# Four output projections with a norm in pieces: the norm of a token tile let out over the following items, and its residual fetched in eight slices

## What is computed

```python
for i in range(DEPTH):                                   # 4 layers
    shift, scale, gate = ada_modulation(c, w_ada[i], b_ada[i])
    h = rms_norm(x, g_norm[i]) * (1.0 + scale) + shift
    ...                                                  # input projection and mixer of layer i: y, z
    out = jnp.einsum('bse,ed->bsd', y * jax.nn.silu(z), w_out)
    x = x + gate * out
return rms_norm(x, g_final), ...
```

## Time and profile before

| | |
|---|---|
| runs, median (lowest to highest) | 2855.18 us (2853.37 to 3117.13) |
| profiled execution, time | 2853.27 us |
| its span, slowest core (core 2) | 2851.7 us (other cores from 2838.4) |
| PE busy | 2253.8 us, 79% |
| DVE busy | 1498.8 us, 53% |
| ACT busy | 778.4 us, 27% |
| mean granted PE clock, 8 cores | 0.913 to 0.920 |
| DMA, mean rate | 75 GB/s |
| chain that ended last, by engine | PE 58%, DVE 19%, ACT 10%, issue 6%, DMA 5% |

### The profile page before, as it was taken

One profiled execution on the slowest core, in us unless ns is written; L12 is line 12 of the kernel. 1 busy time (PEld: TensorE's weight loads), 2 busy tenths in 40 slices (PEclk: granted clock), 3 DMA queues, 4 the chain that ended last, 5 costly groups with the idle time before them and its releaser, 6 DMA issues.

```text
span 2851.7 us, 38831 instructions; the slowest of 8 cores (2838.4 to 2851.7 us)
## 1 busy us (share of the span) xinstructions
PE 2253.8 (79%) x12651; PEld 1200.2 (42%) x12651; DVE 1498.8 (53%) x2600; ACT 778.4 (27%) x1381; POOL 198.4 (7%) x373
## 2 busy tenths in 40 slices
PE   1396899977899999878688888867578687685976
PEld 0142555543455555443345454533243343341543
DVE  1466562233666666533566666567633444757343
ACT  2621233333311111132322222256522322121211
POOL 1001201100010101000000000000000100000000
PEclk9998899988999999988799998988788899897998
DMA  9300727534343433424543334234433421111132
GB/s 185 98 1 4 119 34 130 85 100 103 55 63 50 60 52 52 78 80 125 103 78 78 78 78 78 60 83 116 112 110 115 83 31 27 23 27 15 49 110 86
DMA packets 142851, 215.10 MB, mean 75 GB/s; under 512 B 14560, under 2 KB 83168, under 8 KB 141920
## 3 DMA queue, kind: packets, MB, share of 16 engines
q0 software_dynamic: 50544, 96.00, 22.8%
q1 hardware_dynamic: 92112, 116.63, 13.4%
HBM read 255.18 MB, written 53.40 MB: 108 GB/s over the span
## 4 chain that ended last, share of the span: by engine, by line
PE 58%; DVE 19%; ACT 10%; issue 6%; DMA 5%; POOL 1%; DVEq 1%; ACTq 0%; SPq 0%; POOLq 0%
PE ps L458 37%; PE ps L569 15%; DVE big L1027 4%; ACT big L526 3%; DVE big L516 2%; ACT big L953 2%; DVE big L681 2%; DVE big L1032 2%; ACT big L1012 2%; PE ps L508 2%; PE ps L879 1%; DVE big L915 1%; DMA big<-w_ada 1%; DVE big L524 1%; DMA big<-xbuf 1%
## 5 line engine op out<-in xcount | busy, mean ns | idle before, releaser
L458 PE MATMUL ps<-big 128*128 128x384 bf16 (+4 forms) x7360 | 1417.7, 352 | 206.7 <-ACT big L1012 104.4
L458 PEld LDWEIGHTS ps<-big 128*128 128x128 bf16 x7360 | 723.9, 100 | 841.0 <-issue 305.2
L569 PE MATMUL ps<-big 128*128 128x384 bf16 (+4 forms) x2560 | 522.7, 363 | 20.7 <-DVE big L966 20.7
L569 PEld LDWEIGHTS ps<-big 128*128 128x128 bf16 x2560 | 263.6, 103 | 255.8 <-issue 70.7
L577 DVE SCALAR_TENSOR_TENSOR big<-ps,big 128x384 f32<-128x384 f32 (+3 forms) x192 | 110.2, 582 | 406.6 <-PE ps L569 376.4
L507 ACT ACTIVATE big<-big 128x384 bf16<-128x384 f32 (+4 forms) x200 | 107.9, 554 | 510.1 <-DVE big L577 463.0
L508 PE MATMUL ps<-big 128*128 128x384 bf16 (+4 forms) x200 | 75.3, 397 | 211.3 <-ACT big L507 211.3
L915 DVE TENSOR_TENSOR big<-big,ps 128x384 bf16<-128x384 f32 (+1 forms) x96 | 160.1, 1668 | 106.0 <-ACT big L911 103.0
L526 ACT ACTIVATE big<-big 128x384 bf16<-128x384 f32 (+3 forms) x192 | 131.3, 684 | 94.8 <-DVE big L524 78.6
L1027 DVE TENSOR_TENSOR big<-big 128x398 f32<-128x398 f32 (+11 forms) x200 | 121.9, 610 | 57.6 <-ACT big L1012 42.4
L674 PE MATMUL ps<-big 128*128 128x512 bf16 (+1 forms) x576 | 129.2, 387 | 10.0 <-ACT big L677 5.4
(11 more groups left out here) (105 smaller groups left out, 1678.9 us busy)
## 6 DMA issues: line engine op xcount, KB each, us to landing
big<-w_ada POOLq DMA_DIRECT2D x96, 256.0 KB, 6.6
big<-w_in_b POOLq DMA_DIRECT2D x64, 256.0 KB, 6.6
big<-w_in_c POOLq DMA_DIRECT2D x48, 256.0 KB, 5.4
big<-xbuf SPq DMA_DIRECT2D x7, 1536.0 KB, 8.9
xbuf<-big SPq DMA_DIRECT2D x48, 192.0 KB, 2.0
gbuf<-big SPq DMA_DIRECT2D x16, 548.0 KB, 6.3
big<-gbuf SPq DMA_DIRECT2D x16, 548.0 KB, 4.9
ybuf<-big SPq DMA_DIRECT2D x16, 540.0 KB, 2.7
```

The lines of the kernel that those rows point to most:

```text
L458: ins = h.matmul(out, lhsT=lhs(k), rhs=rhs(k), start=(k == 0), stop=(k == n - 1))
L569: ins = h.matmul(bank(b)[:, 0:w], lhsT=w8[e // 8][:, e % 8, :], rhs=YS[:, e, x0:x0 + w], start=(e == 0), stop=(e == 15))
```

## The change

The L508 of every item now comes two items later. There are four `SQ` buffers, and one buffer `RB` for the reciprocal in place of two. The norm of a tile is a list of nine `chores`: Sqrt and reciprocal, then eight pieces, one a slice (`h_piece`, or `y_piece` in the last projection), each of which also issues the fetch of its slice for tile t + 2. `tick` takes up to three chores after every item, so a norm lasts over three items. The last tile's norm goes on in the first items of the next layer; `proj` empties the list before it reads the last tile. The first two tiles are fetched in eight slices each as well. In layer_c the load of the table `wtab` is deferred by nine items, not three.

```diff
-    RB = [Buf("rb%d" % i, NRM_o + i * 512, 512) for i in range(2)]
-    SQ = [Buf("sq%d" % i, NRM_o + 1024 + i * 256, 512, True) for i in range(2)]
+    RB = Buf("rb", NRM_o, 512)
+    SQ = [Buf("sq%d" % i, NRM_o + 512 + i * 256, 512, True) for i in range(4)]
...
-    def tick():
+    chores = []
+
+    def tick(k=3):
         for e in later:
             e[0] -= 1
         while later and later[0][0] <= 0:
             later.pop(0)[1]()
+        for _ in range(k):
+            if chores:
+                chores.pop(0)()
 
     def flush():
-        while later:
-            later.pop(0)[1]()
+        while later or chores:
+            if later:
+                later.pop(0)[1]()
+            else:
+                chores.pop(0)()
...
+    nsq = [0]
+
     def sumsq(t, d, w):
         q = t % 2
-        k = d % 2
+        S = SQ[nsq[0] % 4]
+        nsq[0] += 1
...
     def rstd(t, w):
+        b = 6 + t % 2
+        s.op("act", lambda h: h.activation(out=RB.v[:, 0:w], in_=bank(b)[:, 0:w], func=AF.Sqrt, bias=EPS, scale=1.0 / D), reads=[], writes=bk(b) + [RB.key])
+        s.op("dve", lambda h: h.reciprocal(out=RB.v[:, 0:w], in_=RB.v[:, 0:w]), reads=[RB.key], writes=[RB.key])
...
+    def h_piece(l, t, d, x0, w, sg):
+        X = XT[t % 2][d]
+        s.op("dve", lambda h: h.tensor_tensor(out=X.v[:, 0:w], in0=X.v[:, 0:w], in1=RB.v[:, 0:w], op=ALU.mult), reads=[RB.key, X.key], writes=[X.key])
+        for (a, b, sq) in sg:
+            s.op("act", lambda h, a=a, b=b, sq=sq: h.activation(
+                out=HT[:, d, 80 + a:80 + b], in_=X.v[:, a - x0:b - x0], func=AF.Identity, scale=gsv(l)[:, d, sq:sq + 1], bias=modv(l)[:, d, sq:sq + 1]),
+                reads=[X.key, "gs%d" % l, "mod%d" % l], writes=["hT.%d" % t])
...
+    def y_piece(t, d, x0, w):
         q = t % 2
-        b = 6 + q
-        R = RB[q]
-        s.op("act", lambda h: h.activation(out=R.v[:, 0:w], in_=bank(b)[:, 0:w], func=AF.Sqrt, bias=EPS, scale=1.0 / D), reads=[], writes=bk(b) + [R.key])
-        s.op("dve", lambda h: h.reciprocal(out=R.v[:, 0:w], in_=R.v[:, 0:w]), reads=[R.key], writes=[R.key])
-        return R
+        X = XT[q][d]
+        s.op("dve", lambda h: h.scalar_tensor_tensor(out=X.v[:, 0:w], in0=X.v[:, 0:w], scalar=gfin[:, d:d + 1], in1=RB.v[:, 0:w],
+                                                     op0=ALU.mult, op1=ALU.mult), reads=[RB.key, X.key, "par"], writes=[X.key])
+        s.dma("sp", "xo%d.%d" % (q, d), yt_d[d][:, x0 - HALO:x0 - HALO + w], X.v[:, 0:w], reads=[X.key], writes=["O.y.%d.%d" % (t, d)])
...
     def make_h(l, t, x0, w, sg):
-        q = t % 2
-        R = rstd(t, w)
+        rstd(t, w)
         for d in range(8):
...
-    def make_y(t, x0, w):
+            h_piece(l, t, d, x0, w, sg)
...
-        if l == 0:
-            src = xt_d[:, :, 80 + x0:80 + x0 + w]
-            rd = []
-        else:
-            src = xbuf[:, :, x0:x0 + w]
-            rd = ["XD.%d.%d" % (t, d) for d in range(8)]
-        s.dma("sp", "xl%d" % q, XTall[q][:, :, 0:w], src.rearrange("d p n -> p d n"), reads=rd, writes=XTK[q])
+        s.dma("sp", "xl%d" % q, XTall[q][:, :, 0:w], xt_d[:, :, 80 + x0:80 + x0 + w].rearrange("d p n -> p d n"), reads=[], writes=XTK[q])
...
+    def load_piece(t, d, x0, w):
+        q = t % 2
+        s.dma("sp", "xi%d.%d" % (q, d), XT[q][d].v[:, 0:w], xbuf[d][:, x0:x0 + w], reads=["XD.%d.%d" % (t, d)], writes=[XT[q][d].key])
+
+    def load_first(t, d, x0, w):
+        q = t % 2
+        s.dma("sp", "xi%d.%d" % (q, d), XT[q][d].v[:, 0:w], xt_d[d][:, 80 + x0:80 + x0 + w], reads=[], writes=[XT[q][d].key])
...
-        load_x(l, 0, *geo[0])
-        load_x(l, 1, *geo[1])
+        fetch = load_first if l == 0 else load_piece
+        for t in range(2):
+            for d in range(8):
+                fetch(t, d, *geo[t])
+
+        def norm(t):
+            x0, w = geo[t]
+            sg = segs(t, lo)
+            chores.append(lambda: rstd(t, w))
+            for d in range(8):
+                def piece(d=d):
+                    if l < 3:
+                        h_piece(l + 1, t, d, x0, w, sg)
+                    else:
+                        y_piece(t, d, x0, w)
+                    if t + 2 < NT:
+                        fetch(t + 2, d, *geo[t + 2])
+                chores.append(piece)
...
-                last = (d == 7)
-
-                def after(st=st, last=last, t=t, x0=x0, w=w, sg=sg):
+
+                def after(st=st, last=(d == 7), t=t):
                     st()
                     if last:
-                        if l < 3:
-                            make_h(l + 1, t, x0, w, sg)
-                        else:
-                            make_y(t, x0, w)
-                        if t + 2 < NT:
-                            load_x(l, t + 2, *geo[t + 2])
-                defer(1 if d < 7 else 2, after)
+                        norm(t)
+                defer(2, after)
...
     def proj(l, idx, t, lo=0):
         x0, x1 = max(TB[t], lo), TB[t + 1]
+        if t == NT - 1:
+            while chores:
+                chores.pop(0)()
...
-        defer(3, lambda: s.dma("pool", "wtab", wt_b.v, wtab_d, writes=["wtab"]))
+        defer(9, lambda: s.dma("pool", "wtab", wt_b.v, wtab_d, writes=["wtab"]))
```

More of the change, by code:

```diff
@@ L501, in segs @@
         return [(x0, SMP, 0), (SMP, x1, 1)]
+    nsq = [0]
     def sumsq(t, d, w):
         q = t % 2
-        k = d % 2
+        S = SQ[nsq[0] % 4]
+        nsq[0] += 1
         b = 6 + t % 2
-        s.op("act", lambda h: h.activation(out=SQ[k].v[:, 0:w], in_=XT[q][d].v[:, 0:w], func=AF.Square), reads=[XT[q][d].key], writes=[SQ[k].key])
-        return lambda: s.op("pe", lambda h: h.matmul(bank(b)[:, 0:w], lhsT=onesb, rhs=SQ[k].v[:, 0:w], start=(d == 0), stop=(d == 7)),
-                            reads=["onesb", SQ[k].key], writes=bk(b))
+        s.op("act", lambda h: h.activation(out=S.v[:, 0:w], in_=XT[q][d].v[:, 0:w], func=AF.Square), reads=[XT[q][d].key], writes=[S.key])
+        return lambda: s.op("pe", lambda h: h.matmul(bank(b)[:, 0:w], lhsT=onesb, rhs=S.v[:, 0:w], start=(d == 0), stop=(d == 7)),
+                            reads=["onesb", S.key], writes=bk(b))
@@ L530, in make_y @@
-    def make_y(t, x0, w):
-        q = t % 2
-        R = rstd(t, w)
-        for d in range(8):
-            X = XT[q][d]
-            s.op("dve", lambda h, X=X, d=d: h.scalar_tensor_tensor(out=X.v[:, 0:w], in0=X.v[:, 0:w], scalar=gfin[:, d:d + 1], in1=R.v[:, 0:w],
-                                                                  op0=ALU.mult, op1=ALU.mult), reads=[R.key, X.key, "par"], writes=[X.key])
-            s.dma("sp", "xo%d.%d" % (q, d), yt_d[d][:, x0 - HALO:x0 - HALO + w], X.v[:, 0:w], reads=[X.key], writes=["O.y.%d.%d" % (t, d)])
+            h_piece(l, t, d, x0, w, sg)
@@ L865, in build_more @@
                     build(*build_q.pop(0))
-        nsq = [0]
+        nsc = [0]
         def conv(c):
@@ L886, in conv @@
                 s.op("act", lambda h, b=b, y=y, bias=bias: h.activation(out=y, in_=bank(b)[:, 0:YPH], func=AF.Identity, bias=bias), reads=["par"], writes=bk(b) + ["yp.%d" % c])
-                q = SQC[nsq[0] % 6]
-                nsq[0] += 1
+                q = SQC[nsc[0] % 6]
+                nsc[0] += 1
                 s.op("dve", lambda h, y=y, q=q: h.tensor_tensor(out=q.v, in0=y, in1=y, op=ALU.mult), reads=["yp.%d" % c], writes=[q.key])
```

## The result

| | before | changed |
|---|---|---|
| runs beside each other, us | 3117.13, 2855.18, 2853.37, 3112.19 | 2696.07, 2893.49, 2960.29, 2675.09 |
| median of these four | 2983.68 | 2794.78 |
| ratio of the executions compared | 1 | 0.9409 (95% interval 0.925 to 0.9568) |
| repeated later on another chip | 2856.81 | 2680.4; ratio 0.9391 (0.9371 to 0.941) |

The change makes the kernel 6% faster. The measured median, 2794.78 us, lies outside the range that was given, 2645 to 2740.

A forecast was written before the change was run, and what follows sets the result against it. Bound: PE's waits at the sum-of-squares matmul in the projections, plus slow clock after them. 19.4 + 113 + 36 + 3 + 2 - 1 = 172.4 off 2853.3 gives 2680.9, stated as 2682; range 2645 to 2740.

The forecast's parts named there:

- first sum of squares of a projection: PE's stalls before a projection's first L508, 19.4 us in sum, all taken away by fetching the tile in slices.
- boundary stalls left: At the 16 tile boundaries of the projections, 21.7 us of 134.9 stay and 113 us go.
- slow clock left in the projections: Of 49 us of slow clock after stalls in the projections, 12.6 stay and 36 come back.
- preamble: Before the first projection, four SQ buffers remove the gaps between pairs of Squares: 3 us gained.
- layer c: Its 15.15 us wait for the last tile's burst: PE gets its bank earlier, later pieces delay the next; gain 2.
- layer d: Its wait for the last tile's piece 7 grows by up to 4.7 us, mostly made up since DVE limits it; loss 1.
- rival (c): Fourth projection: SP's store-and-fetch chain stops being hidden above a 3.5 us link; at 5.4 us landings, 2739; chance 0.09.
- (e): Slower than before: SP chain lateness, 24 x link + 35 - 120, reaches 172 at a link of 10.7 us; chance 0.03.
- The trace does not agree: Clock step: PE at granted clock 1.00 from 800 to 1150 us, so no 13/16 cut; 36 us of clock come back.
- The rival that priced the level: Clock cut to 13/16 in the now dense projections: 112 us more, 2794; chance 0.03.
- the stalls would vanish wholly: Rival at the tile boundaries: no stalls left and the clock stays up, 2650; chance 0.10.
- ACT and DVE stay the bound: Rival at the tile boundaries: 5 us at each of 16 and the clock still drops, 2765; chance 0.11.

The follow-up runs named there:

- the burst experiment: The changed kernel with the sum of squares three items later, and the last tile's norm ahead of layer d in one burst: 2649.61 us median, ratio 0.9283.

## Why the prediction was right, and where it failed

**The bound and the walk: right.** The rows of each step:

| step | said | measured |
|---|---|---|
| first sum of squares of a projection | 19.4 us gone | 17.7 (1.71 left in the second) |
| boundary stalls left | 21.7 us | 18.4: 4.95, 4.95, 4.64, 3.84 |
| one projection's four | 3.0, 1.1, 0, 2.0 | 2.53, 0.79, 0, 1.63 |
| slow clock left in the projections | 12.6 us | 493.6 - 484.4 = 9.2 |
| the four projections | about 520 us | 513.7 |
| preamble | 3 us gone | the first projection starts at 545.0 to 549.0 on six cores (before 549.0 to 552.6), in the repeat at 548.3 to 550.7: 4 and 2 us |
| layer c | gain 2 | 683.9 to 682.0 on the slowest cores, but 679 to 684 over all eight, before and after: no gain shown |
| layer d | loss 1, the wait up by up to 4.7 | the wait up by 4.8; 437.6 to 438.5, in the repeat 437.9 to 440.1 over the cores |
| link of the SP chain | 3.0, hidden up to 3.5 | 3.30, hidden |

Taken on the slowest cores, the last column adds up: 2853.3 less 174.1 in the projections, 4 in the preamble, 2 in layer c and plus 1 in layer d is 2674, and the fastest execution took 2675.09; the repeat's median is 2680.4. The terms of the preamble and of layer c are no larger than the spread of the cores, so that the sum closes to 1 us is in part luck. The figure of 2682 was good to 0.3% for executions without a loss of clock.

Two slips of the working change little. Half of what the earlier trace rows shows behind the stall of 3.24 us is 1.26 us and not 1.4, and the late slice of rival (c) is 59 us by the formula of (e), which makes it 2741 and not 2739. The sum also gives all eight stalls the same loss of clock; measured, three of them make 4.9 of the 9.2 us on this core and the other five nothing, as the last section shows.

In layer c PE gets its bank sooner, and a second wait now stands behind the first; that the pieces delay the next tile's Sigmoid is my reading of it:

```profile
1322.71 6.57 PE L466 MATMUL ps<-big 128*128 128x512 bf16 x16 [7.14 <-DVE big L939]
...
1334.17 13.44 PE L466 MATMUL ps<-big 128*128 128x416 bf16 x64 [4.89 <-DVE big L939]
```

7.14 and 4.89 us in place of 15.15. In layer d the wait is 17.27, 4.8 more:

```profile
2141.99 21.30 PE L466 MATMUL ps<-big 128*128 128x416 bf16 x104 [17.27 <-ACT big L531]
```

Here most of it was made up, as predicted: in layer d PE waited 101.4 us for the layer's copies where the kernel before waited 104.4, and was busy 319.5 us for 320.4, which gives back 3.9 of the 4.8. That it is so because DVE limits that layer was a guess, and the burst experiment speaks against it as a rule: with three items of delay nothing was given back. Why the two differ is open.

**The step that failed: "The trace does not agree: this core shows nothing of it in 350 us of dense matmul".** From one window of one execution I concluded that the clock is 1.00 whenever PE is dense, gave the 13/16 level 0.03, and built the range for executions at full clock only. What the runs showed in its place: two of the four executions took 2893 and 2960 us, 8 and 10% more than the middle of the other two, with one die at a mean granted clock of 0.86 and 0.81. The runs of before had warned of it: 3117.13 stood among its three, 9% above the others. A range for the median of a few executions has to take such an execution in, and mine did not.

The level exists in the kept traces as well. Three of the thirteen profiled executions have it in stretches without a pause of PE, each time on both cores of a pair (0 and 1, 2 and 3, 4 and 5) at once. The changed kernel has it on cores 2 and 3 in layer a and on cores 0 and 1 from about 2600 us on, in the fourth projection, where it cost 10 us (133.6 against 123.9). The kernel with the norm in one burst has it on cores 2 and 3 in layer b, from about 740 to 880 us; its core 2 and then its core 5:

```profile
800.00:900.00 100.00, 100.00 (x510) 50.67 (x509) 55.76 (x122) 14.79 (x28) 9.49 (x18) 0.83 0.35 48
```

```profile
800.00:900.00 100.00, 100.00 (x615) 55.33 (x614) 66.55 (x149) 17.86 (x34) 12.13 (x23) 1.00 0.44 64
```

The Trainium skill (TensorE: Matmul & The Clock Gate, Part 1: The HAM clock gate) names 13/16, which is 0.8125, for the whole die once three of its cores run dense matmuls. The trace agrees in the level but not in the condition: the changed kernel's core 3 stays at 0.97 to 1.00 in four dense projections with the same program on the other cores, and where cores 2 and 3 have 0.81 in layer a, cores 0 and 1 of their die have 1.00. No trace was kept of the executions of 2893 and 2960 us. Their spans go by pairs too (2888 and 2892, 2783 and 2788 us in the first), which fits, but that they had the same level, and what sets it off, stays open. The rival that priced the level, 2794, assumed it in the projections alone; that the median, the middle between two kinds of execution, fell on that figure is chance.

**The other rivals.** That the stalls would vanish wholly (2650) was wrong for two items of delay and right for three. That ACT and DVE stay the bound did not happen: ACT is over-full only for two items and then has time. The SP chain stayed hidden, but only by 0.2 us a link against the limit of 3.5 that the sum gave; the landings are 2.8 us where they were 2.4, with loads now between the stores:

```profile
yt<-big SPq DMA_DIRECT2D x24, 192.0 KB, 2.8
```

The fixed 2.0 us that the prediction takes from the Trainium skill (DMA: Bandwidth & Descriptors, Anatomy of one DMA) are given there for DMAs issued through GpSimd. These stores are issued by SP, so its 2.5 us are an estimate for another path; the two medians measured, 2.4 and 2.8 us, lie beside it.

## What to carry to other kernels

When one engine must wait for a result that passes through two others, walk the boundary with the three queues side by side, with durations of the trace: what is queued ahead of that result on each, and when the waiting engine gets there. Cut the burst ahead of it, and move the wait later by enough items that the walk ends at zero; here three items instead of two gave another 25 us for one changed number. Where the end of a burst is itself awaited, as ahead of layer d, leave the burst whole; that gave another 6 us. And look at the spread of the run times before you give a range for their median.

## What the runs showed that was not expected

A granted clock of 0.81 turns up on pairs of cores in some executions and not in others, for up to some 140 us without a pause, with the other cores at 1.00 in the same stages.

A stall of some 2.5 us can cost another 1.7 us in clock, or nothing. At 1216.07 above the item behind it takes 4.44 us in place of 2.76. In the two profiles of the changed kernel, all eight cores of each, there are 48 stalls of 2.2 to 2.5 us in the first three projections: behind 33 of them the next item takes 4.1 to 4.4 us, behind 15 it takes 2.76. Core 3 lost clock behind all three in the first profile and behind none in the second. Behind the shorter stalls, 150 of 0.3 to 1.8 us with an item behind them, no item is slower than at full speed; behind the one of 1.71 us above, the 432-wide item takes 3.08, where 3.10 with its L519 is the full price. So a part of what is left over differs from core to core and from run to run with the same stalls.

And with no pause the four projections ran at 483.8 us, within 0.2% of the sum of their items.
